# A decoder step on one core: GpSimd leaves two stage barriers, the window-state copies move between stages, and the prompt rows are loaded by tiles

## The reference, cut to what matters

```python
def reference(x_prompt, x_sample, cache_k_sb, cache_v_sb, page_table, state_k_win, state_v_win, w_in, w_out, ...):
    qa, ka, va, qd, kd, vd = split_projections(x_prompt, w_in)      # (512 x 1024) @ (1024 x 3072)
    qd, kd = rope(qd, pos_p), rope(kd, pos_p)
    o_sb_p = sb_prompt(qa, ka, va, sb_logit_bias)                   # stick-breaking attention, 8 heads
    o_dil_p = merge_by_denominator(*dilated_bands(qd, kd, vd))      # dilated windows, 8 heads
    y_prompt = finish_layer(x_prompt, o_sb_p, o_dil_p, ...)
    ...                                                             # the same for the 32 sample rows, over
                                                                    # paged past keys and the window state
    kc = jnp.concatenate([state_k_win, kd_s], axis=1)
    vc = jnp.concatenate([state_v_win, vd_s], axis=1)
    return (y_prompt, y_sample, ..., kc[:, n_buf + T - keep_s:], vc[:, n_buf + T - keep_s:])

def finish_layer(x, o_sb, o_dil, w_out, ln1_g, ln1_b, peer_wq, ...):
    mixed = jnp.concatenate([o_sb, o_dil], -1) @ w_out
    h1 = layer_norm(DN_ALPHA * x + mixed, ln1_g, ln1_b)
    f = peer_ffn(h1, ...)             # queries h1 @ peer_wq, the best 16 of 16384 experts for each of 8 heads
    return layer_norm(DN_ALPHA * h1 + f, ln2_g, ln2_b)
```

## Time and profile before

| | us |
|---|---|
| three runs | 2494.16, 2484.43, 2496.20 |
| their median | 2494.16 |
| the profiled execution | 2485.89 |
| its span, first to last instruction | 2484.1 |
| PE busy in the span | 2298.1 (93%) |
| DVE busy | 1548.5 (62%) |
| ACT busy | 940.5 (38%) |
| POOL busy | 390.8 (16%) |

### The profile page before, as it was taken

One profiled execution on the slowest core, in us unless ns is written; L12 is line 12 of the kernel. 1 busy time (PEld: TensorE's weight loads), 2 busy tenths in 40 slices (PEclk: granted clock), 3 DMA queues, 4 the chain that ended last, 5 costly groups with the idle time before them and its releaser, 6 DMA issues.

```text
span 2484.1 us, 37894 instructions
## 1 busy us (share of the span) xinstructions
PE 2298.1 (93%) x12921; PEld 1896.2 (76%) x12921; DVE 1548.5 (62%) x3167; ACT 940.5 (38%) x1432; POOL 390.8 (16%) x370
## 2 busy tenths in 40 slices
PE   7997887999999788998999879999999999999996
PEld 7996674666666436985577779999999999999995
DVE  3342331344434423769898877777777777777777
ACT  3224643445444401223356623333333333333332
POOL 0001000000000000000000043333333333333330
PEclk9998888989989888999999989999999999999998
DMA  4226985766666574303355699999999999999982
GB/s 129 87 88 204 304 270 186 233 194 208 209 212 215 171 255 143 97 25 97 99 197 183 235 344 322 314 314 313 313 315 313 311 312 311 314 313 312 311 294 82
DMA packets 224063, 568.20 MB, mean 229 GB/s; under 512 B 18017, under 2 KB 96418, under 8 KB 221282
## 3 DMA queue, kind: packets, MB, share of 16 engines
q1 hardware_dynamic: 174946, 327.75, 39.9%
q0 software_dynamic: 49024, 239.23, 27.7%
HBM read 528.24 MB, written 105.12 MB: 255 GB/s over the span
## 4 chain that ended last, share of the span: by engine, by line
PE 71%; DVE 6%; DMA 4%; SPq 2%; ACT 2%; issue 2%; DVEq 0%; ACTq 0%
PE psum L2067 21%; PE psum L2055 16%; PE psum L1842 6%; PE psum L1563 3%; PE psum L2045 3%; PE psum L999 3%; PE psum L1865 3%; PE psum L1071 2%; PE psum L1053 2%; PE psum L989 2%; PE psum L1419 2%; PE psum L1021 2%; DMA sample<-in_cache_v_sb_dram 1%; DMA peer<-in_ln_b_dram 1%; DMA peer<-in_peer_wq_dram 1%
## 5 line engine op out<-in xcount | busy, mean ns | idle before, releaser
L2067 PE MATMUL psum<-expert_parts 128*128 128x512 f32 x2304 | 550.5, 395 | 0.0
L2067 PEld LDWEIGHTS psum<-expert_parts 128*128 128x128 f32 x2304 | 427.0, 189 | 86.3 <-issue 0.8
L2055 PE MATMUL psum<-h_parts,expert_parts 128*128 128x384 f32 x2304 | 444.2, 341 | 2.9 <-DVE expert_parts L2172 1.5
L2055 PEld LDWEIGHTS psum<-h_parts,expert_parts 128*128 128x128 f32 x2304 | 402.9, 189 | 10.9 <-issue 1.8
L2119 ACT ACTIVATE expert_parts<-peer 128x1024 fp32r<-128x1024 f32 x128 | 135.8, 1061 | 359.1 <-PE psum L2067 322.2
L2172 DVE TENSOR_TENSOR expert_parts<-psum,expert_parts 128x512 fp32r<-128x512 f32 x192 | 132.7, 691 | 151.4 <-ACT expert_parts L2113 151.4
L2215 DVE SCALAR_TENSOR_TENSOR kept<-experts,kept 128x1024 f32<-128x1024 f32 x160 | 205.0, 1281 | 5.3 <-DVE kept L2205 3.0
L2030 POOL DMA_INDIRECT experts<-in_peer_v_dram,kept x160 | 188.5, 1178 | 70.1 <-issue 47.5
L1842 PE MATMUL psum<-h_whole,gate_table 128*128 128x384 f32 x512 | 179.0, 493 | 13.8 <-ACT gate_table L1894 13.8
L1326 DVE TENSOR_TENSOR sample_parts<-sample,sample_parts 128x512 fp32r<-128x512 f32 x128 | 85.1, 690 | 157.5 <-ACT sample_parts L1179 157.0
L400 PE MATMUL psum<-projection_parts 128*128 128x256 f32 (+1 forms) x1440 | 173.5, 282 | 3.8 <-DVE projection_parts L506 3.8
(11 more groups left out here) (281 smaller groups left out, 3261.9 us busy)
## 6 DMA issues: line engine op xcount, KB each, us to landing
peer<-in_peer_v_dram SPq DMA_DIRECT2D x128, 512.0 KB, 5.2
peer<-in_peer_u_dram SPq DMA_DIRECT2D x96, 512.0 KB, 5.4
sample<-in_cache_k_sb_dram SPq DMA_DIRECT2D x128, 256.0 KB, 3.1
sample<-in_cache_v_sb_dram SPq DMA_DIRECT2D x128, 256.0 KB, 2.9
out_dram<-in_state_k_win_dram POOLq DMA_DIRECT2D x8, 4088.0 KB, 35.6
out_dram<-in_state_v_win_dram POOLq DMA_DIRECT2D x8, 4088.0 KB, 33.8
gates_dram<-gate_table SPq DMA_DIRECT2D x12, 2048.0 KB, 7.1
experts<-gates_dram SPq DMA_DIRECT2D x32, 768.0 KB, 6.9
```

Of the source, the lines that this page charges most:

```text
L2055: last = pe.matmul(bank(6)[:, 0:ND], lhsT=u_t[s][:, a, k, :], rhs=h1_r[:, b, k, 0:ND], start=(k == 0 and n == 0), stop=(k == KD - 1 and n ...
L2067: last = pe.matmul(bank(2 * t + half), lhsT=weight[s][:, a, t * P:(t + 1) * P], rhs=v_r[s][:, b, half * 512:(half + 1) * 512], start=(firs ...
```

## The change

Four things are changed.

- The first barrier (`WITHOUT_POOL = (1,)`): POOL neither drains nor waits there, and all later barriers count one arrival less. So POOL goes on from its last store of projections to the wait for `counts`. ACT now waits itself, before it writes `o_t`, for the store of the dilated keys, whose source lies there.
- The barrier between the two prompt attentions is gone for all engines. In its place PE waits for all logits and exponents of the stage before its first dilated scores, and for all copied outputs before its first transposes; DVE waits for the weighted values of seven heads before it writes the first dilated logits, and of eight before the second.
- The 16 window copies were issued 7, 4, 3 and 2 at the start of stages 2, 3, 5 and 6; now they are issued 11, 0, 0 and 5.
- `sq` is loaded first, and the prompt rows in four DMAs of 512 KB, each with a semaphore of its own.

```diff
+        WITHOUT_POOL = (1,)
         def end_stage(eng):
             name = eng.engine
             stage[name] = stage.get(name, 0) + 1
+            if eng is nc.gpsimd and stage[name] in WITHOUT_POOL:
+                return
             eng.drain().then_inc(over, 1)
-            eng.wait_ge(over, 5 * stage[name])
+            eng.wait_ge(over, 5 * stage[name] - len([n for n in WITHOUT_POOL if n <= stage[name]]))
...
+        X_IN = ("x_prompt_in", "x_in_1", "x_in_2", "x_in_3", "small_in")
...
-            sp.dma_start(x_nat[:, 0:4, :], x_rows).then_inc(sem("x_prompt_in"), 16)
+            sp.dma_start(sq, square).then_inc(sem("square_in"), 16)
+            for t in range(4):
+                sp.dma_start(x_nat[:, t, :], x_rows[:, t, :]).then_inc(sem(X_IN[t]), 16)
             sp.wait_ge(sem("tail_cleared"), 1)
             sp.dma_start(x_nat[0:NS, 4, :], xs_rows).then_inc(sem("small_in"), 16)
-            sp.dma_start(sq, square).then_inc(sem("square_in"), 16)
...
             for t in range(NT):
-                pe.wait_ge(sem("x_prompt_in" if t < 4 else "small_in"), 16)
+                pe.wait_ge(sem(X_IN[t]), 16)
...
-        MOVES = (7, 4, 3, 2)
+        MOVES = (11, 0, 0, 5)
...
-        for engine in programs:
-            programs[engine].append(end_stage)
-
-
         PT_AT = (0, 1, 3, 6)
...
             def scores(h):
                 if h >= 1:
                     pe.wait_ge(sem("dl_logits"), 4 * h)
+                else:
+                    pe.wait_ge(sem("sb_logits"), H)
+                    pe.wait_ge(sem("sb_exponents"), H)
...
                 if h >= 1:
                     pe.wait_ge(sem("dl_turned"), h)
+                else:
+                    pe.wait_ge(sem("sb_out_copied"), H)
...
                 if h >= 2:
                     dve.wait_ge(sem("dl_turn"), h - 1)
+                else:
+                    dve.wait_ge(sem("sb_out"), H - 1 + h)
...
         def _(act):
+            act.wait_ge(sem("k_dil_out"), (1 + DB) * 16)
             for u in range(8):
```

## The result

The changed kernel is slower: a median of 2506.76 us over 11 runs (2501.59 to 2522.74) against 2494.16 us for the kernel before (2484.43 to 2499.94, 11 runs on the same chip). The two medians differ by 12.6 us, a ratio of 1.0051; the recorded comparison of the runs puts the ratio at 1.007, with a 95% interval from 1.0052 to 1.0089, which is 13 to 22 us. The forecast was 2506.9, slower by 12.7. The profiled execution took 2506.03 us with a span of 2504.2, 20.1 more than the span of the kernel before.

The account below looks back on a forecast made before the run. PE, with 71% of the chain, was taken to bound the kernel, stage after stage. -7.0 - 9.4 - 10.0 - 0.1 + 39.2 = +12.7 us on the median 2494.16 makes 2506.9; range 2486 to 2517.

Parts of the forecast that it names:

- The loss in the query stage: Query stage: five copies delay the load of group 2 and PE stands still; loss 39.2 us, between 37.8 and 43.4.
- 96 and 114 packets: Query stage, 970 to 990 us: DMA engines alternate between load (0.10 MB) and copies (6.41 MB) packet by packet.
- the first and the third rival: Query stage: load not held up further, 2467.7 us, chance 0.07; stall partly hidden, loss some 28, 2495.7 us, chance 0.04.
- The gain in the output projection: Output projection: without copies the norm's row lands early and PE has no gap; gain 10.0 us, between 8.4 and 10.5.
- The barriers: After the projections, without POOL: gain 7.0 us (4.6 to 7.8); between the attentions, barrier removed: gain 9.4 (7.7 to 10.7).
- the second head: Dilated attention: the second head's scores, also slow in the trace, can give up to 1.5 us more.
- The eleven copies: Third barrier: eleven copies in one piece take 147.7 us from 209.4, end at 357.1 and stay hidden.
- the second rival: Third barrier: the eleven copies hold it; at 14.0 us each the sum is +18.4, 2512.6 us; chance 0.07.
- the margin: Third barrier: copies end at 357.1, ACT arrives at 358.4, so they stay hidden by 1.3 us only.
- nothing of x can be split before the clearing ends: Start, prompt rows: DVE clears buffers until 13.08 us, then splits x without a gap for 5.20 us.
- a gain of 0.1: Start, prompt rows: earlier arrival in four DMAs gains 0.1 us, between 0 and 0.5.

Follow-up runs that it names:

- The move alone: Kernel before with three of its sixteen copies moved from the output projection to the query stage, (7, 4, 0, 5), nothing else: 2520.20 us, ratio 1.0116.
- the waiting copies: Changed kernel with GpSimd issuing the query stage's five copies only after the last load of `peer_wq` has landed: 2468.81 us, ratio 0.9923 to the kernel before.
- the three copies: Changed kernel with three of its five query-stage copies back at the start of the output projection, (11, 0, 3, 2): 2477.94 us, ratio 0.9944 to the kernel before.
- the barrier of four engines: Changed kernel with a barrier of four engines, without GpSimd, put back between the two prompt attentions: 2512.12 us in one execution.

## Why the prediction was right

The loss in the query stage (+39.0 measured, +39.2 forecast) and its cause are shown. The load of group 2 landed after 66 us where it took 27.72 (+38.3), and the first block behind it took 9.55 us where it took 8.87 (+0.7). The move alone brings the loss, the waiting copies take it away, and packets stand near one to one at four sizes. The Trainium skill, "DMA: Bandwidth & Descriptors", section "Queues, rings and completion order", says that a DMA engine goes round its queues and changes at the end of a packet. The traces of all four agree, from 327 packets against 348 to 1604 against 1822. What the forecast read from 96 and 114 packets held; only a packet of the copies is 53 KB in the records, not 65, which no term of the sum used. With 0.33 MB of the load in 58 us, and the landing after 66 us, the first and the third rival are out.

The gain in the output projection (-10.2 to -10.0) held in size and mechanism: the norm's row lands in 5.0 us, PE has no gap, and the stall comes back with the three copies.

The barriers gave -6.6 and -9.1 to -7.0 and -9.4. The first is short because `counts` takes 7.28 us beside the stores, not the 6.85 that I took. For the second the size met the forecast in this pair, partly by luck: over all profiles the step gains 5.3 to 9.5. The first logits came 7.4 us earlier, counted from DVE's first logits of the stage before; the forecast had 7.7 to 9.2. The other 1.7 us are the second head, which the forecast priced at up to 1.5. They do not belong to the barrier: from the first logits to the second it took 5.94 and 4.25 us in this pair, but also 5.94 in a kernel without the barrier (the waiting copies, granted clock 0.65 from 304 to 308, where the changed kernel had 1.00) and 4.25 in one with it (the move alone). That most of the gain is GpSimd's drain only the barrier of four engines showed.

The eleven copies ended at 357.5 (forecast 357.1), which puts the second rival out. They began 2.4 us later than forecast and took 145.7 us in place of 147.7. ACT didn't arrive at 358.4, as forecast, but at 363.9: the margin was 6.4 us instead of 1.3.

What was off lay in stretches that I held unchanged: 7.0 of the 7.4 us by which the profiled pair (20.1) lies over the forecast (12.7). The prompt rows: the step "nothing of x can be split before the clearing ends" is true, but "a gain of 0.1" was wrong, since early transposes put PE and ACT out of step with DVE. In this pair the main matmuls start 1.3 us later and the projections end 2.0 later, by the medians of all profiles 0.6 and 1.1. The end of the dilated stage lost 3.3, where two heads ran at the low clock level. It is not the missing barrier, since those heads are as slow with the barrier back and in the kernel with the move alone. Nor is it shown to be the change at all: from the second dilated logits to the sample stage took 56.1 us in the profile of the kernel before and 59.4 in the changed one, but also 58.9 with the move alone, whose program up to there is the kernel before, and 56.5 in the changed kernel with copies of 8 KB. What brings the fall forward stays open. The sample stage's 0.8 and the 0.95 at the end are within what those stretches vary by themselves.

So the median met the forecast to 0.2 us partly by luck. The profile that the terms were read from lies 8.3 us under the median of its kernel, and stretches without an edit differ by some us from one execution to the next; the forecast held them at nothing. That the medians differ by 12.6 us, where the profiled pair differs by 20.1, is nothing that its sum explains. The recorded interval is 13 to 22 us, and the forecast's +12.7 lies just under it.

## What to carry to other kernels

When a large copy and a small-packet load use the same DMA engines, look at packets, not at bytes: queues that take packets one for one let the large one through and the other stand, so issue the copy behind the last load that an engine waits for. Before a copy is moved to where it looks hidden, list the loads that it will lie beside and what waits for each. Where GpSimd has DMAs under way, a barrier with its drain waits until they have landed, so a barrier is cheap only without it, or ahead of its issues (here 1.0 to 2.3 us without GpSimd).

## What the runs showed that I had not expected

A DRAM to DRAM copy lost more than half of its rate when cut into pieces of 4 KB (138 GB/s in place of 324 with no load beside it). With the load beside it both queues together moved 146 GB/s with 4 KB, 249 with 8 KB, and with 16 KB (328) as much as with whole copies (327).

GpSimd's drain grew with the copies in flight: 52.5 us with four, 91.7 with seven, 141.2 with eleven, and 324.2 with eleven in pieces of 4 KB.

A stage of 500 us with no edit in it varied by 12 us between executions of these kernels.
